# Uneven rows in one weight transfer per expert, an earlier start of the weight stream, and three stores on another queue

## The reference, cut to what matters

```python
h = rms_norm(x, norm_ffn_w)
probs = softmax(h @ w_router)                 # (tokens, 16)
aff, idx = lax.top_k(probs.T, cap)            # cap = 64 prompt tokens, 32 sample tokens per expert
xe = h[idx]
hid = silu(xe @ w_gate[e]) * (xe @ w_up[e])   # 1024 -> 2816
ye = (hid @ w_down[e]) * aff[..., None]       # 2816 -> 1024
out[idx] += ye ; y = rms_norm(x + out)
```

## Time and profile before

| | us |
|---|---|
| median of the runs | 2447.57 |
| span of the profiled execution | 2445.6 |
| outside the span, to the median | 2.0 |
| TensorE busy in the span | 2395.3 |
| VectorE, ScalarE, GpSimd busy | 1074.5, 514.2, 305.4 |
| mean granted TensorE clock | 0.993 |
| moved by DMA over the span | 707 MB |

### The profile page before, as it was taken

How to read it: one execution, slowest core, us unless ns; L and a number is a source line. 1 busy time by engine, 2 the same in 40 slices (tenths; PEclk the granted TensorE clock), 3 DMA queues, 4 the chain that set the end, 5 groups by cost and what they waited for, 6 DMA issues and landing times.

```text
span 2445.6 us, 49821 instructions
## 1 busy us (share of the span) xinstructions
PE 2395.3 (98%) x22095; PEld 1636.4 (67%) x22095; DVE 1074.5 (44%) x2029; ACT 514.2 (21%) x1059; POOL 305.4 (12%) x418
## 2 busy tenths in 40 slices
PE   9899999999999999999999999999999999999996
PEld 9798999899898888845655544455455455455453
DVE  6989889888987634421121221112112121211213
ACT  5445444444534412100000000000000000000001
POOL 0313332441341000000000000000000000000001
PEclk9899999999999999999999999999999999999998
DMA  5133333223335536399999999999999999999996
GB/s 183 56 125 98 98 106 125 89 95 126 110 117 209 205 138 230 118 400 413 410 412 416 415 411 420 415 411 415 416 418 409 419 415 408 421 407 416 420 409 238
DMA packets 88486, 707.00 MB, mean 289 GB/s; under 512 B 11632, under 2 KB 15856, under 8 KB 51408
## 3 DMA queue, kind: packets, MB, share of 16 engines
q1 hardware_dynamic: 65360, 628.93, 63.4%
q0 software_dynamic: 14272, 56.60, 7.4%
q10 hardware_dynamic: 8640, 18.29, 2.0%
HBM read 669.72 MB, written 34.06 MB: 288 GB/s over the span
## 4 chain that ended last, share of the span: by engine, by line
PE 79%; DMA 17%; DVE 3%; issue 1%; ACT 1%; POOL 0%; ACTq 0%; POOLq 0%; DVEq 0%
PE p_gu L2435 28%; PE pp L1131 17%; DMA raw<-in_w_e 14%; PE p_y L2453 8%; PE pp L1339 6%; PE pp L1175 5%; PE p_y L2456 3%; PE pp L1368 2%; PE p_z L2456 2%; PE pdg L1226 2%; DMA raw_first<-in_w_e 2%; PE off_banks L1209 1%; PE ptr L1193 1%; PE pp L1447 1%; PE off_banks L1223 1%
## 5 line engine op out<-in xcount | busy, mean ns | idle before, releaser
L2435 PE MATMUL p_gu<-raw,xT 128*32 128x512 f32 (+1 forms) x8304 | 863.0, 558 | 11.7 <-DMA raw<-in_w_e 10.9
L2435 PEld LDWEIGHTS p_gu<-raw,xT 128*32 128x32 f32 x8304 | 366.9, 110 | 418.4 <-issue 321.9
L2331 DVE SCALAR_TENSOR_TENSOR tg<-tg,p_gu 128x256 f32<-128x256 f32 (+1 forms) x144 | 57.4, 399 | 1084.5 <-ACT tg L2295 1080.1
L2453 PE MATMUL p_y<-raw,hidT 128*32 128x384 f32 x3744 | 432.2, 486 | 0.0
L2295 ACT ACTIVATE tg<-p_gu 128x256 f32<-128x256 f32 (+1 forms) x144 | 52.7, 366 | 1283.5 <-PE p_gu L2435 1283.5
L2456 PE MATMUL p_y<-raw,hidT 128*32 128x256 f32 x1248 | 320.2, 379 | 0.0
L1131 PE MATMUL pp<-h_hi,wx_hi 128*128 128x256 f32 (+1 forms) x832 | 295.1, 355 | 0.5 <-ACT fo L717 0.5
L1131 PE MATMUL pp<-h_hi,wx_lo 128*128 128x256 f32 (+1 forms) x832 | 281.5, 338 | 0.0
L1131 PE MATMUL pp<-h_lo,wx_hi 128*128 128x256 f32 (+1 forms) x832 | 280.9, 338 | 0.0
L2453 PEld LDWEIGHTS p_y<-raw,hidT 128*32 128x32 f32 x3744 | 153.9, 110 | 87.9 <-issue 56.6
L2456 PE MATMUL p_z<-raw,hidT 128*32 128x256 f32 x624 | 185.6, 379 | 0.0
(11 more groups left out here) (283 smaller groups left out, 3315.0 us busy)
## 6 DMA issues: line engine op xcount, KB each, us to landing
raw<-in_w_e SPq DMA_DIRECT2D x185, 2048.0 KB, 38.1
raw<-in_w_e SPq DMA_DIRECT2D x58, 1536.0 KB, 35.6
raw_first<-in_w_e SPq DMA_DIRECT2D x23, 2048.0 KB, 39.0
w_raw<-in_w_x SPq DMA_DIRECT2D x48, 512.0 KB, 3.5
dec<-acs POOLq DMA_DIRECT2D x48, 512.0 KB, 4.8
raw<-in_w_e SPq DMA_DIRECT2D x16, 1024.0 KB, 38.0
w_raw<-in_w_g SPq DMA_DIRECT2D x24, 512.0 KB, 3.5
g_tab<-gx POOLq DMA_DIRECT2D x8, 1152.0 KB, 5.9
```

Of the source, the lines that this page charges most:

```text
L2331: dve.scalar_tensor_tensor(out=tg[:, r % 2, 0:w], in0=tg[:, r % 2, 0:w], scalar=1.0, in1=p[:, 0:w], op0=ALU.add, op1=ALU.mult).then_inc(s_ ...
L2435: mm = pe.matmul(p_gu[g][quad(q), 0:w], xT[:, e % 2, k * SLOTS + 32 * g:k * SLOTS + 32 * (g + 1)], slot[:, at:at + w], start=(k == 0), sto ...
L2453: pe.matmul(y_first[half][quad(g), :], hidden(g), w[:, half * 3 * P:(half + 1) * 3 * P], start=first, stop=last)
```

## The change

A chunk may be issued in several row ranges, each with its own transfer on the same semaphore. For one chunk per expert, the last gu chunk of the second block of 8, these are rows 0 to 111, 112 to 119 and 120 to 127. PE waits for the count of all transfers that the slot has seen. SP no longer stores the last tile of `xa`, the two sample tiles of `h2` and the sample's probabilities; ACT does, between its own work. After the prompt's probabilities SP waits only for `s_o` and issues chunks 2 to 6 together.

```diff
+def row_parts(c):
+    kind, b, i = chunk(c)
+    if kind == "gu" and i == KS - 1 and b % NB == 1:
+        return (0, 112), (112, 120), (120, P)
+    return ((0, P),)
+
+def landed(c):
+    return 16 * sum(len(row_parts(before)) for before in range(c % RAW, c + 1, RAW))
...
-    sp.dma_start(raw[c % RAW][:, 0:w], src).then_inc(s_raw[c % RAW], 16)
+    for lo, hi in row_parts(c):
+        sp.dma_start(raw[c % RAW][lo:hi, 0:w], src[lo:hi, :]).then_inc(s_raw[c % RAW], 16)
...
                     sp.dma_start(probs_of(0, NTP), prob[:, 0:NTP]).then_inc(m_pr, 16)
+                    break
                 sp.wait_ge(s_x2, t + 1)
...
-                if t == NT - 1:
-                    sp.wait_ge(s_o, NT)
-                    load_part(sp, A, e_raw, s_eraw, 2)
...
-            for t in range(NTP, NT):
-                sp.wait_ge(s_h, t + 1)
-                sp.dma_start(h2[t * P:(t + 1) * P, 0:D], hh[:, t % 2, :]).then_inc(s_h2[t % 2], 16)
-            sp.wait_ge(s_pr, 2)
-            sp.dma_start(probs_of(NTP, NT), prob[:, NTP:NT]).then_inc(m_pr2, 16)
...
             for t in range(NTP, NT):
                 row_square(t)
                 row_turned(t)
+            t = NT - 1
+            act.wait_ge(s_x2, NT)
+            act.dma_start(xa[t * P:(t + 1) * P, :], x2[:, t % 2, :]).then_inc(s_xa[t % 2], 16)
             for t in range(NTP, NT):
                 softmax_exp(t)
+            for t in range(NTP, NT):
+                act.wait_ge(s_h, t + 1)
+                act.dma_start(h2[t * P:(t + 1) * P, 0:D], hh[:, t % 2, :]).then_inc(s_h2[t % 2], 16)
+            act.wait_ge(s_pr, 2)
+            act.dma_start(probs_of(NTP, NT), prob[:, NTP:NT]).then_inc(m_pr2, 16)
...
-            for c in range(3, 7):
+            sp.wait_ge(s_o, NT)
+            for c in range(2, 7):
                 load_part(sp, A, raw, s_raw, c)
             sp.wait_ge(s_xt, 1)
+            sp.wait_ge(s_pr, 2)
...
-                pe.wait_ge(s_raw[c % RAW], 16 * (c // RAW + 1))
+                pe.wait_ge(s_raw[c % RAW], landed(c))
```

More of the change, by code:

```diff
@@ L2098, in mixer @@
                 (*((sem, 16 * NTP // 2) for sem in s_h2), (m_pr, 16), (s_idx, 1), (s_o, NT)),
-                (hh, sel, picks, p_first, p_s, s_h, s_sel, s_picks, s_ia, s_xa, s_h2))
+                (hh, sel, picks, p_first, p_s, s_h, s_sel, s_picks, s_ia, s_xa, s_o, s_pr))
 def experts(nc, block, signals, cleared, mixed, prompted, picked, A, cst, raw, s_raw, h2, xa, idx, idx_p, outs):
@@ L2139, in tiles @@
             return ap.rearrange("p (k s) -> p k s", k=KD)
-        hh_rows, sel, picks, p_first, p_s, s_h, s_sel, s_picks, s_ia, s_xa, s_h2 = picked
+        hh_rows, sel, picks, p_first, p_s, s_h, s_sel, s_picks, s_ia, s_xa, s_o, s_pr = picked
         prompt_rows = p_h[:, 0:KD * CAPS[0]].rearrange("p (k s) -> p k s", k=KD)
```

## The result

The kernel after takes 2659.05 us (median of six runs, 2646.79 to 2674.13) against 2447.33 us for the kernel before, measured on the same chip: 1.0876 times as long, 95% interval 1.0855 to 1.0897. It is 211.7 us slower, where 2436.6 was forecast with a range up to 2478.

The account below looks back on a forecast made before the run. The stream of expert weights was taken to bound the kernel, with 21.7 us of waits to be had. Rows -8.5, start -2.5 and 0 for the rest make -11.0 us, from 2447.6 to 2436.6 us, range 2430 to 2478.

Parts of the forecast that it names:

- What bounds the kernel: Experts' part: TensorE runs at the pace of the weight stream; a faster stream can give up to 21.7 us.
- a row of 16 KB costs its engine 0.63 us: Cut chunks: price of one row, from 414 GB/s over 16 engines, used to count each engine's work.
- the rows term: Cut chunks, 16 experts: moving one row per engine from the late half to the early one gives -8.5 us.
- The rival of slow pieces: Eight-row pieces share an SBUF entrance; gain gone at 0.92 us a row, 2453 to 2499 us; chance 0.24.
- the sign of slow pieces: GB/s dip once per expert, landings well above 42 us, `raw` waits above 21.7 us, the first before 1430.
- The late half: End of the weight stream: half of the 16 engines finishes 17 us behind, and TensorE waits for it.
- which half the small pieces go to: Eight-row pieces go to the early engines; rival that they go to the late ones: 2455 us, chance 0.08.
- the instruction packets: Instruction queue's 16 KB packets, 7.6 per expert, likely cause the lag, about 1.0 us per expert; inferred.
- The start term: Start of the weight stream: earlier issue of chunks 2 to 6 fills empty DMA time, -2.5 us, at most 3.0.
- ACT's stores: Four transfers moved to ACT: its idle time before the exponentials and the prompt's columns covers the issues; price 0.
- SP's extra issues: Two more issues per expert on SP, 10.6 us of a queue that waits for TensorE: costs nothing.
- the later gather: Prompt gather meets the fuller stream, 0 to 3.8 us longer, say 2; price 0 while the stream never runs dry.

Follow-up runs that it names:

- experiment 1: Kernel after with every chunk whole, early issue and ACT's stores kept: 2445.53 us, ratio 0.9992; also kernel before with the row cut alone: 2663.22 us.
- experiment 2: Kernel after with pieces of 112 and 16 rows: 2652.58 us, ratio 1.0833; with two pieces of 64 rows: 2654.07 us, ratio 1.0839.
- experiment 3: Kernel after with the special chunk in two transfers of all 128 rows and half the columns each: 2446.13 us, ratio 0.9996.
- experiment 6: Kernel after with seven eighths of the special chunk's columns whole, the last eighth in 16 pieces of eight rows four apart: 2490.24 us, ratio 1.017.
- experiment 5: Kernel after with the special chunk in eight pieces of 16 rows: 2668.97 us, ratio 1.0906.
- experiment 8: Transfers alone, no reference computed: six-chunk streams, the fourth whole or cut by rows, engine halves in or out of step; whole 32.2 us in step.

## Why the prediction was wrong, point by point

- **What bounds the kernel: right.** The stream sets the time nearly one for one: 203 us lost in it are 211.7 us of kernel.
- **The step that failed: "a row of 16 KB costs its engine 0.63 us", and with it the rows term of -8.5 us.** It counted the rows of each engine and took the price of a row as fixed, whatever transfer it came in. Measured, the cut costs +13.3 us per expert (213.5 / 16, experiment 1 against the kernel after), where the count gives -0.5. What brings the price is the cut by rows: halves of 64 cost as much (experiment 2), columns nothing (experiment 3), and every cut by rows that was tried cost time. By itself a transfer of 112 rows takes 9.9 us where the count says seven eighths of 7.7. That the engines share an entrance to SBUF is the reading that fits these numbers; no row names an entrance.
- **The rival of slow pieces had the right kind of mechanism, in the wrong place and too small.** It charged only the 16 rows of the 8-row pieces, and reached 2499. In the traces the piece of 112 rows is slow too (9.9 us alone, where 128 rows take 7.7), and so is a half of 64. The rival got a chance of 0.24; what was held against it was "it concerns 16 of 288 chunks". The dip shows why that doesn't count. In its 20 us at half rate 20 x 218 = 4.4 MB pass, twice the cut chunk's 2.1 MB, so the chunks in flight beside the cut one are held up with it.
- **What the prediction named as the sign of slow pieces came, all four:** the dip once per expert, landings of up to 49.09 us in the chain (42 was named), waits of 157.8 us, the first of them before 1430.
- **The late half, and which half the small pieces go to: right.** The packets show two halves that part by 1.3 us per expert, to 20 us at the end, where the shares gave 17, and they stay together in the kernel after (experiment 6). So the shift of rows did what it was meant to do, and the -8.5 us were lost in the price of the cut, not in its direction. The way that experiment 6 moves load between the halves costs more than the lag as well. Moving it without a cut by rows was not tried. That the instruction packets cause the lag stays inferred.
- **The start term: right as far as it can be measured.** -2.5 us foretold, about -2 measured with an interval that reaches 0, share 0.94 at 1030 to 1035 against "near 0.9".
- **ACT's stores, SP's extra issues, the later gather: right at 0.** The gather went from 7.4 to 10.6 us in experiment 1 and 10.2 after, longer by 3.2 and 2.8 where 0 to 3.8 was said, and the kernel of experiment 1 is not slower. Two issues in the place of one cost nothing in experiment 3.

Still open: why a few engines fall behind after some cuts, and what of the 13.3 us goes to them. Why more and smaller pieces hardly cost more in the kernel (experiment 5: +15 us over 16 experts), where by themselves they cost 6 us more each (experiment 8: +11.4 against +5.2 in step). And how much of the 42.9 us of experiment 6 goes to where the small pieces are written and how much to their count.

## What to carry to other kernels

Don't cut a large transfer by its rows when it runs in a full stream. Cut it by columns, which was free here, and keep all 128 partitions in each piece. Before a balance is made by counting rows per engine, ask whether a row still costs the same in the new shape, and time that shape once by itself and once in a stream: single transfers would have shown 112 rows at 9.9 us against 7.7 for 128. When a stream slows, read share and GB/s together, since the engines counted as busy at half their rate here.

## What the runs showed of the hardware

- The DMA share was 1.03 at 216 GB/s and 1.01 at 414: the engines' busy time rose with the time of a packet.
- A transfer of 64 neighbouring rows with 1 MB takes as long (7.3 us) as one of 128 rows with 2 MB (7.7); over the even rows it takes 5.4. The Trainium skill, "SBUF — State Buffer", section "Door 1: The DMA port swizzle", ties groups of partitions to shared ports, so that fewer groups means less bandwidth; these three numbers agree in kind. The Trainium skill, "SBUF — State Buffer", section "Can I just issue two DMAs to hit both halves?", says that two transfers to two halves don't make up for one over all partitions. Here they cost 5.2 to 6.7 us more per 2 MB in a stream by itself, which agrees, and up to 14.6 with the halves of the engines out of step.
- The Trainium skill, "DMA: Bandwidth & Descriptors", section "The descriptor swizzle", has each engine on a port of its own in a transfer of 128 partitions. That fits the cut by columns at no cost and the price of every cut by rows. No row here names a port.
- A cut in 64 and 64 rows cost 5.2 us in a stream with its engines in step and 14.6 us with one half 5.5 us late (experiment 8). In the kernel it cost 7.2 us in the first two experts and 14.1 in the thirteenth and fourteenth (counted from 0).
- In the kernel before one half of the 16 engines falls behind by 1.3 us per expert, evenly, to 20 us after 16 experts (packets, experiment 6).
